# A hybrid MLA and SSD layer on one core: convolution tiles as plain products, and the SSM decay differences on ScalarE instead of VectorE

## The reference, cut to what matters

```
proj = u @ w_in
q_lat, kv_lat, z_attn, xbc, dt_raw, z_ssm = split_last(proj, IN_SPLITS)   # 384, 320, 1024, 1536, 16, 1024
...
xbc = jax.nn.silu(causal_depthwise_conv(xbc_raw, conv_w, conv_b))         # 4 taps
...
a_cum = jnp.cumsum(A, axis=2)                                             # within a chunk of 128 tokens
seg = a_cum[:, :, :, None] - a_cum[:, :, None, :]
tri = jnp.tril(jnp.ones((CHUNK, CHUNK), dtype=bool))[:, :, None, None]
decay = jnp.exp(jnp.where(tri, seg, -jnp.inf))
cb = jnp.einsum('bclgn,bcsgn->bclsg', Cc, Bc)
y_diag = jnp.einsum('bclsgr,bcsgrp->bclgrp', cb[..., None] * decay, X)
decay_to_end = jnp.exp(a_cum[:, :, -1:] - a_cum)
```

## Time and profile before

| | us |
|---|---|
| median of 3 runs | 995.63 (993.08 to 997.70) |
| profiled execution | 992.91 |
| its span | 991.1 |
| TensorE busy | 895.7 (90%), mean granted clock 0.966 |
| VectorE busy | 759.0 (77%) |
| ScalarE busy | 473.5 (48%) |
| GpSimd busy | 380.6 (38%) |
| chain of waits | PE 50%, DVE 25%, issue 6%, ACT, DMA and POOL 5% each |

### The profile page before, as it was taken

The page is one execution under the profiler, slowest core; times in us unless marked ns, Lnnn a source line. Parts: engine busy times, 40 slices in busy tenths (PEclk is TensorE's granted clock), DMA queues, the critical chain, the costliest instruction groups (busy, mean ns, idle before and its releaser), DMA issues.

```text
span 991.1 us, 13509 instructions
## 1 busy us (share of the span) xinstructions
PE 895.7 (90%) x4593; PEld 737.5 (74%) x4593; DVE 759.0 (77%) x1117; ACT 473.5 (48%) x785; POOL 380.6 (38%) x228
## 2 busy tenths in 40 slices
PE   4999996799668898899888999999999999999996
PEld 3788775587557676677666888889889778888884
DVE  6999889868688889888883676667676768548977
ACT  3644333343343554344534766667567654323431
POOL 1051458888445545564534332333143200001412
PEclk9999997999879999999988999999999999999998
DMA  9965312533524553355438142143134319833522
GB/s 295 314 213 157 123 42 85 170 92 102 175 66 139 172 174 105 99 176 168 155 100 270 44 138 89 54 138 127 50 114 149 134 57 385 311 131 128 204 73 85
DMA packets 126034, 143.78 MB, mean 145 GB/s; under 512 B 11205, under 2 KB 98598, under 8 KB 125990
## 3 DMA queue, kind: packets, MB, share of 16 engines
q1 hardware_dynamic: 125584, 142.38, 43.7%
q10 hardware_dynamic: 406, 0.84, 0.4%
HBM read 103.28 MB, written 36.77 MB: 141 GB/s over the span
## 4 chain that ended last, share of the span: by engine, by line
PE 50%; DVE 25%; issue 6%; ACT 5%; DMA 5%; POOL 5%; SPq 4%; DVEq 0%; ACTq 0%; POOLq 0%
PE bank L932 12%; PE bank L934 12%; PE bank L933 12%; DVE dec L2036 8%; PE bank L1214 3%; ACT dec L1550 2%; SPq L470 2%; DMA wraw<-in_w_in 2%; DVE cdv L2030 2%; PE bank L1199 2%; PE bank L1203 2%; PE bank L1202 2%; PE bank L1200 1%; POOL diff_lo L804 1%; PE bank L1201 1%
## 5 line engine op out<-in xcount | busy, mean ns | idle before, releaser
L932 PE MATMUL bank<-uspan,wh 128*128 128x512 f32 x352 | 145.9, 414 | 8.4 <-ACT xra L1440 2.0
L934 PE MATMUL bank<-uspan,wl 128*128 128x512 f32 x352 | 139.1, 395 | 0.0
L814 POOL TENSOR_TENSOR wl<-wraw,wh 128x512 fp32r<-128x512 f32 x60 | 97.1, 1628 | 76.5 <-ACT wh L1435 76.5
L933 PE MATMUL bank<-uspan,wh 128*128 128x512 f32 x304 | 119.4, 393 | 0.0
L932 PE MATMUL bank<-owh,mxh 128*128 128x512 f32 x256 | 100.2, 391 | 0.0
L934 PE MATMUL bank<-owh,mxl 128*128 128x512 f32 x256 | 99.8, 390 | 0.0
L933 PE MATMUL bank<-owl,mxh 128*128 128x512 f32 x256 | 99.7, 389 | 0.0
L932 PEld LDWEIGHTS bank<-uspan,wh 128*128 128x128 f32 x352 | 67.5, 192 | 27.8 <-issue 11.5
L2036 DVE SCALAR_TENSOR_TENSOR dec<-dec,bdt,mask_ls 128x128 f32<-128x128 f32 x128 | 83.8, 715 | 1.1
L932 PE MATMUL bank<-diff_hi,wh 128*128 128x512 f32 x144 | 63.1, 438 | 21.6 <-ACT ost L1440 9.7
L896 POOL TENSOR_TENSOR yn<-yn,lgb 128x512 f32<-128x512 f32 x7 | 11.1, 1579 | 182.8 <-ACT yn L1792 182.8
(11 more groups left out here) (245 smaller groups left out, 2441.2 us busy)
## 6 DMA issues: line engine op xcount, KB each, us to landing
wraw<-in_w_in SPq DMA_DIRECT2D x33, 512.0 KB, 5.4
owr<-in_w_out SPq DMA_DIRECT2D x32, 512.0 KB, 4.4
wada<-in_w_ada SPq DMA_DIRECT2D x16, 512.0 KB, 6.0
dec<-acum_scratch SPq DMA_DIRECT2D x32, 256.0 KB, 4.0
proj_scratch<-ost SPq DMA_DIRECT2D x16, 512.0 KB, 4.6
stg<-conv_scratch SPq DMA_DIRECT2D x7, 832.0 KB, 4.4
xin<-in_x SPq DMA_DIRECT2D x8, 512.0 KB, 6.0
conv_scratch<-cvb SPq DMA_DIRECT2D x8, 512.0 KB, 3.0
```

What stands on the lines that cost most here:

```text
L814: pool.tensor_tensor(wl[:, at], part, wh[:, at].bitcast(F32), ALU.subtract).then_inc(pair_split, 1)
L932: pe.matmul(dst, ah, bh, start=start, stop=False, skip_group_check=running)
L933: pe.matmul(dst, ah, bl, start=False, stop=False, skip_group_check=running)
L934: return pe.matmul(dst, al, bh, start=False, stop=stop, skip_group_check=running)
```

## The change

All twelve convolution tiles become plain tiles (`NORMAL` from 10 to 18), and only the eight z pairs keep the seven products. So the four convolution pairs' sums, splits, copies and additions go, and eight `proj_tile` of 48 matmuls come. Every convolution tile but the last two now uses the set `b`. In the SSD, ScalarE computes the fall of the sum as Relu(column - row), with the column as the bias, and Exp of its negative; it is at least 0 and so the exponential at most 1, also where the mask applies. The mask becomes a factor of 1 or 0 on C.B, which is multiplied in place in its PSUM bank and read from there. To keep that bank, y goes to banks 4 and 5 and the new states to banks 6 and 7. The decay to the chunk's end is copied from the last column of the Exp's result, not computed apart.

```
-NORMAL = 10
-LATE = NORMAL - 6
-PAIRS_XBC = (CONVT - LATE) // 2
-PAIRS = PAIRS_XBC + CHUNKS
+NORMAL = 6 + CONVT
+PAIRS = CHUNKS
+RAW_BASE = (16 * (NORMAL // 2 - 1), 16 * (NORMAL // 2))
...
-            return "b" if j < LATE or (j - LATE) % 4 < 2 else "a"
+            return "a" if j >= LAST_X else "b"
...
 @@ SP
+            for tile in range(11, NORMAL):
+                load_tile(tile % 2, W_XBC + (tile - 6) * P, tile - 1)
+                store_conv(tile - 11)
+                if tile == 14:
+                    for i, t in enumerate((2, 3, 4, 0, 1)):
+                        sp.wait_ge(lat_ready, i + 1)
+                        sp.dma_start(scr[t], qk[:, t, :]).then_inc(y_out, 16)
+            store_conv(7)
             load_pair(0)
...
 @@ GpSimd
-            pool.affine_select(mask_ls[:], mask_ls[:], pattern=[[1, P]], compare_op=ALU.is_ge, fill=NEG,
+            pool.affine_select(mask_ls[:], mask_ls[:], pattern=[[1, P]], compare_op=ALU.is_ge, fill=0.0,
...
+            for tile in range(3, NORMAL):
                 split_tile(tile)
-            split_difference(0)
-            split_tile(NORMAL - 1)
-            split_difference(1)
-            split_difference(2)
-            for q in range(PAIRS_XBC + 1):
-                split_pair(q)
+                if 10 <= tile < 13:
+                    split_difference(tile - 10)
+            split_pair(0)
...
 @@ TensorE
+            for tile in range(8, NORMAL):
+                proj_tile(tile)
...
-            for q in range(PAIRS_XBC):
-                for i in range(7):
-                    product(i, q, q % 2 == 1)
...
-                        d = [bk(6 + r % 2)[64 * q:64 * q + 64, i * P:(i + 1) * P] for q in range(2)]
+                        d = [bk(4 + r % 2)[64 * q:64 * q + 64, i * P:(i + 1) * P] for q in range(2)]
...
-                    mm = pe.matmul(bk(4 + g), bdt[:, B0 + g * P:B0 + (g + 1) * P], xdte[:, g * HB:(g + 1) * HB],
+                    mm = pe.matmul(bk(6 + g), bdt[:, B0 + g * P:B0 + (g + 1) * P], xdte[:, g * HB:(g + 1) * HB],
...
 @@ ScalarE
+            for tile in range(6, NORMAL):
+                j = tile - 6
+                if j == LAST_X:
+                    act.wait_ge(xra_clear, 1)
+                elif 2 <= j < LAST_X:
+                    act.wait_ge(conv_done, j - 1)
...
+                evac(tile, conv_in(j)[:, 3:3 + S])
+                if tile + 3 < NORMAL:
+                    high_tile(tile + 3)
+                if j >= 1:
+                    conv_silu(j - 1)
...
+            def fall(r, c):
+                act.wait_ge(bdt_ready, c + 1)
+                act.wait_ge(exa_ready, 4 * c + r + 1)
+                for i in range(4):
+                    part, h = dec[:, r, i * P:(i + 1) * P], AC0 - DT0 + 4 * r + i
+                    a = act.activation(part, part, ACT.Relu, bias=bdt[:, h:h + 1], scale=-1.0)
+                a.then_inc(arg_ready, 1)
+
             def exp_decay(r, c):
                 act.wait_ge(arg_ready, 4 * c + r + 1)
-                act.activation(dec[:, r, :], dec[:, r, :], ACT.Exp).then_inc(dec_ready, 1)
+                act.activation(dec[:, r, :], dec[:, r, :], ACT.Exp, scale=-1.0).then_inc(dec_ready, 1)
...
 @@ VectorE, ssd_round
-                dve.tensor_tensor(cdv[:, 1, 4 * r:4 * r + 4], dec[:, r, P - 1:HB:P],
-                                  bdt[:, AC0 - DT0 + 4 * r:AC0 - DT0 + 4 * r + 4], ALU.subtract).then_inc(rest_ready, 1)
+                dve.wait_ge(dec_ready, 4 * c + r + 1)
+                dve.tensor_copy(cdv[:, 2, heads], dec[:, r, P - 1:HB:P]).then_inc(rest_ready, 1)
                 dve.wait_ge(rest_ready, 4 * c + r + 1)
-                for i in range(4):
-                    h = 4 * r + i
-                    arg = dve.scalar_tensor_tensor(...)
-                arg.then_inc(arg_ready, 1)
                 ex = decays(r).rearrange("p (h l) -> p h l", h=4)
                 dve.tensor_tensor(ex, ex, stg[:, 10 + g, :].unsqueeze(1).to_broadcast([P, 4, P]), ALU.mult)
-                dve.wait_ge(dec_ready, 4 * c + r + 1)
                 de = dec[:, r, :].rearrange("p (h l) -> p h l", h=4)
-                dve.tensor_tensor(de, de, cbs[:, g * P:(g + 1) * P].unsqueeze(1).to_broadcast([P, 4, P]),
+                dve.tensor_tensor(de, de, bk(7)[:, g * P:(g + 1) * P].unsqueeze(1).to_broadcast([P, 4, P]),
                                   ALU.mult).then_inc(g_ready, 1)
...
 @@ VectorE, chunk
-                dve.tensor_copy(cbs[:], bk(7)[:, 0:2 * P])
+                cb = bk(7)[:, 0:2 * P].rearrange("p (g l) -> p g l", g=2)
+                dve.tensor_tensor(cb, cb, mask_ls[:].unsqueeze(1).to_broadcast([P, 2, P]), ALU.mult).then_inc(cb_masked, 1)
```

More of the change, by code:

```diff
@@ L442, in build_layer @@
         LAST_X, LAST_Y = CONVT - 2, CONVT - 1
-        SILU_COUNT = {**{j: j + 1 for j in range(LAST_X)}, LAST_X: LAST_X + 3, LAST_Y: LAST_X + 4}
+        SILU_COUNT = {**{j: j + 1 for j in range(CONVT - 1)}, LAST_Y: CONVT + 1}
         @block.sync
@@ L494, in load_pair @@
             def load_pair(q):
-                if isinstance(q, int) and q < PAIRS_XBC:
-                    cols = [W_XBC + (LATE + 2 * q + p) * P for p in range(2)]
-                else:
-                    cols = [address(w + (q - PAIRS_XBC) * P) for w in (W_ZATT, W_ZSSM)]
+                cols = [address(w + q * P) for w in (W_ZATT, W_ZSSM)]
                 src = [w3[:, :, bass.ds(col, P)] for col in cols]
@@ L1493, in _ @@
-            high_difference(2)
-            for i in range(3):
-                high_product(i, 0)
-            act.wait_ge(conv_done, 1)
-            evac(8, conv_in(2)[:, 3:3 + S])
+            for tile in range(6, NORMAL):
[4 more added lines that the diff above has]
+                    act.wait_ge(conv_done, j - 1)
+                if tile == 7:
+                    act.wait_ge(sq_ready, 1)
+                evac(tile, conv_in(j)[:, 3:3 + S])
[3 more added lines that the diff above has]
+                    conv_silu(j - 1)
+                if tile == 7:
+                    act.wait_ge(sums_mm, 2)
+                    for g in range(2):
+                        act.activation(rb[:, g, :], bank[2 + g][:].rearrange("p a b -> p (a b)"), ACT.Sqrt,
+                                       bias=rcst[:, 3:4], scale=1.0 / (384, 256)[g]).then_inc(root_ready, 1)
+                if tile == 8:
+                    act.wait_ge(kr_gate_out, 48)
+                    act.wait_ge(diff_sum, 3)
+                if 8 <= tile < 11:
+                    high_difference(tile - 8)
+                if tile == NORMAL - 2:
+                    high_product(0, 0)
+                    high_product(1, 0)
+                    high_product(2, 0)
@@ L1590, in chunk @@
                     high_product(2, q + 1)
+                fall(2, c)
+                if more:
                     high_product(3, q + 1)
+                fall(3, c)
                 exp_decay(2, c)
@@ L1597, in chunk @@
                 if more:
-                    act.activation(cdv[:, 2, :], cdv[:, 1, :], ACT.Exp).then_inc(dte_ready, 1)
                     high_product(4, q + 1)
@@ new lines, in _ @@
+            for j in range(LAST_Y):
+                dve.wait_ge(proj_evac, 2 * j + 14)
+                conv(j)
+                if j in (1, 2):
+                    inverse_root(j - 1)
+                if 3 <= j < 6:
+                    for t in ((2, 3), (4, 0), (1,))[j - 3]:
+                        latent_norm(t)
+                if j == 8:
+                    dve.wait_ge(y_out, LATENTS_OUT)
+                    for p in range(2):
+                        ins = dve.memset(xra[:, p, 0:3], 0.0)
+                    ins.then_inc(xra_clear, 1)
+                    dve.wait_ge(xra_clear, 1)
@@ L2027, in ssd_round @@
+            dve.wait_ge(proj_evac, 2 * NORMAL - 1)
+            conv(LAST_Y, 0, P)
+            dve.wait_ge(silu_done, LAST_X + 1)
+            dve.tensor_copy(stg[:, LAST_X, :], conv_out(LAST_X)[:, 0:P])
+            dve.wait_ge(silu_done, LAST_X + 2)
+            dve.tensor_copy(stg[:, LAST_Y, :], conv_out(LAST_Y)[:, 0:P]).then_inc(stage_ready, 1)
+            dve.wait_ge(proj_evac, 2 * NORMAL)
+            conv(LAST_Y, P, S)
+            dve.wait_ge(conv_done, CONVT + 1)
             def ssd_round(r, c):
```

161 lines of the change are left out of this document (29 added, 132 removed).

## The result

The changed kernel takes 963.7 us (median of 4 runs, 960.2 to 966.4); the kernel before took 994.4 beside it (4 runs, 992.4 to 997.7). The ratio is 0.969, 95% interval 0.964 to 0.973. The forecast was 959 with a range of 944 to 976. The profiled execution took 966.42 us, which makes it the slowest of the four; against the 992.9 of the one before it is 26.5 us shorter, where the working said 34.

What follows compares the result with a forecast made beforehand. TensorE was busy in 90% of the span, its chunk waits running through VectorE, which GpSimd locks. From the profiled 992.9 us, 992.9 - 20 - 2 - 10 - 2 = 959, range 944 to 976.

Steps and rivals of the forecast that it cites:

- Part 1: Convolution stage: eight plain tiles for four pairs run without stops, bringing turn_stage(0) from 260.6 to 240.6, -20.0 us.
- Part 2: Chunk 0: ScalarE computes the decays, so product 4 waits less for the copy of product 2; -2 us.
- weights land near 248.6 ... copy 257.7: Chunk 0, ScalarE's sequence from the weights' landing to the copy of product 2, done at 257.7 against 278.8.
- Part 3: Chunks 1 to 6: decays move from VectorE to ScalarE's Relus, period 30.3 for 32.0 us, -10 us in all.
- waits for its DMA until T + 3.4 to 4.4: Chunks 1 to 6: ScalarE's high part ahead of the first Relu waits for weights until 3.4 to 4.4 us after turn_stage's start.
- slow rival: Chunks: Relus stand behind a weight load landing 5 us later; period 35.8, total 994 or 1004; chance 0.04.
- to about 18: Chunks 1 to 6: VectorE's busy time per chunk falls from 27.8 us to about 18, no bound by load.
- Part 4: Last chunk: the last g_ready moves from 21.6 to about 19.5 us after turn_stage's start, -2 us.
- The tiles aren't fed: Rival, convolution tiles: SP queue or a locked convolution stops TensorE for 10 to 15 us; 969 to 974; chance 0.07.
- TensorE becomes the bound: Rival, six chunks: the period falls to 28.1 us, saving 23 for 10; total 946; chance 0.18.
- The chunks give nothing: Rival, chunks: the wait only moves from VectorE to ScalarE, period stays 32.0, last chunk 0; total 971; chance 0.17.
- The change doesn't do what it says: Rival, decay rounds: a Relu needing another table adds two loads of 1.28 us a round; within the slower case's 0.04.

Runs made afterwards that it cites:

- the fastest variant: Changed kernel with GpSimd's last difference split behind VectorE's last convolution piece and ScalarE's decay rounds ahead of next-pair high parts in all chunks but the last: 936.3 us, ratio 0.941.

## Why the prediction was right, and where it was not

The time was inside the range and the sign right; two of the four terms hold, two don't. The misses don't cancel, and some luck is in how near the number came: the sum was made for the profiled execution, and that took 966.4, 7.4 above the forecast, while the median of 963.7 is only 4.7 above it.

*Part 1, right.* Turn_stage(0) at 239.6 for 240.6, tiles without a stop, the stage load as the last wait (0.55). What I did not walk is what the shorter stage does to the piece behind it.

*Part 2, wrong sign: +2.6 for -2.* The term "weights land near 248.6 ... copy 257.7" (its parts as listed add up to 258.3) took VectorE's last convolution piece for free; the load landed at 254.2, and the copy of product 2 was done at 262.8. In the kernel before, it ran at 256.9 to 262.1 with GpSimd mostly quiet; in the change GpSimd's splits for pair 0 stand right under it, and it takes 11.2 us for 5.2. ScalarE's SiLU, the first copy, the store and the next weight load (issued at 250.1, landed at 254.2) all follow it. That GpSimd's splits are the cause of the longer piece, and of most of the first stop behind it, is shown by the run in which GpSimd waits (5.2 us again, and 2.60 for 8.43). They are not all that chunk 0 lost: there it still takes 41.0 us, since the wait for product 4's addition comes in their place, and only with ScalarE's four rounds ahead of the high parts as well does it fall to 31.6. The gain from ScalarE computing the decays is there (3.6 in the run with that part alone), and the tiles take 6.9 from chunk 0. So of the 21 us that the tiles win ahead of chunk 0, 14 are left behind it.

*Part 3, right in sign and in what bounds the chunk, too large: -6.7 for -10.* The Relus cost what I had worked out (eight in 2.44, so 1.22 a round for 1.25: 0.31 apart, which is the upper bound of 0.39 less the overlap of 0.08). Rounds 2 and 3 did disappear under the products. Round 1 was forecast at 13.3 to 14.3 behind T; in the six chunks it is at 14.5, 15.7, 12.7, 14.1, 12.9 and 14.3. The failed step is "waits for its DMA until T + 3.4 to 4.4": ScalarE passes that wait at T + 5.0, 6.2, 3.2, 4.7, 3.4 and 4.8, and TensorE's second y round starts 9.4 to 9.5 us behind it in every one of the six. The stops of these chunks come to 17.1 us, 2.85 a chunk, where a period of 30.3 with 28.1 busy leaves 2.2. That is the mechanism of my slow rival at a fraction of its size: in the four chunks where ScalarE passes after T + 4.4, the stops are 3.0 to 3.9 us, in the other two 1.7 and 1.8. The run with the Relus ahead of the load shows that their place matters; it took 6 to 7 us off. I also took `lanes` at its old price in VectorE's load: "to about 18" a chunk is 20.6, since `lanes` now waits for GpSimd (1406 ns for 681). And the stop of "about 2.5 before the second y round" is split: it is 2.75 ahead of the first and 1.17 ahead of the second in the long chunk, 1.68 ahead of the second in the short one. Why the load itself comes early and late in turn, I read only from the trace: in a short chunk (345.95) ScalarE's z gates wait for VectorE (2.37), the z store goes out at 372.2 and the next load's issue begins at 373.6, only 1.0 ahead of the next turn_stage; in a long one (312.38) it begins at 343.3, 2.6 ahead. In the longest chunk (312.38) ScalarE also waits longer from the issue (7.4 us, in the others 5.7 to 6.2). No run tests either.

*Part 4, right in size:* 36.7 for 38.7.

*The rivals.* "The tiles aren't fed" did not happen. "TensorE becomes the bound" holds in no chunk of the changed kernel, though the short ones come within 1.9 us; it is nearly true of the fastest variant. "The chunks give nothing" is out, by 6.7 us. "The change doesn't do what it says" is out: the traces have 25 table loads on ScalarE each, before and after (the prediction counted 17; what matters is that none is new).

*The clock.* I allowed 0.7 a chunk for it, for a low clock "in about every other chunk"; by the windows it was in four of the six before the change (0.95), at some 1.4 us of TensorE's time each. TensorE's busy time in chunks 1 to 6 is 28.2 as a mean, against 27.0 at clock 1.00, so 1.2, about as much as in the kernel before (169.4 in the six, and 168.9 now). The variant with all rounds early has 27.0, and the difference to the changed kernel in these chunks, 19.0, is 7.1 of busy time and 11.9 of stops.

## What to carry to other kernels

On an engine with one order of work, put what waits for a transfer or another engine's late result behind what the critical engine waits for: moves of that kind on ScalarE, with one added wait on GpSimd and no computing instruction added or removed, gave 28 us where the whole change had given 31. When a stage gets shorter, look again at what ran at its end in the quiet: its last piece may now lie under another engine's busy stretch. Taking away one wait may only uncover the next, as in chunk 0, so follow the stops after each step. And a wait that TensorE has is worth more than its length where the clock falls behind it, so price stops at the low clock too.
